# Six tiles held at the head of each stage, the seventh after them: other orders around five norms of a two-block transformer kernel

## The chip, the cores and the metric

The kernel runs on one core of one Trainium2 chip. The metric is the time of one execution on the device in microseconds (us), as the median of several runs. A profile is one further execution, recorded by the hardware profiler. All times below are microseconds.

## The reference

512 tokens of 1024 values, f32, pass through two transformer blocks. What matters here is that each stage begins with an RMS norm, whose result enters one wide matrix product:

```python
def rms_norm(x, g):
    x32 = x.astype(jnp.float32)
    y = x32 * lax.rsqrt(jnp.mean(x32 * x32, axis=-1, keepdims=True) + EPS)
    return (y * g.astype(jnp.float32)).astype(x.dtype)
...
        xn = rms_norm(h, g_mix_pre[i])
        z = xn @ w_in[i]
        conf_ab, q, k, v, f_logit, sc_h, sc_b, sc_c, pool_v = jnp.split(z, SPLIT_IDX, axis=-1)
...
        h = h + rms_norm(mix, g_mix_post[i])
        hn = rms_norm(h, g_mlp_pre[i])
        ff = jnp.square(jax.nn.relu(hn @ w_up[i])) @ w_down[i]
        h = h + rms_norm(ff, g_mlp_post[i])
        gate = jax.nn.sigmoid(rms_norm(h, g_ple_pre[i]) @ w_ple_gate[i])
        e = (p[i] @ w_ple_proj[i]) * gate
        h = h + rms_norm(e, g_ple_post[i])
```

The first mixer holds a forgetting attention, a gated depthwise convolution, a short convolution and a pooling. The second block has a norm, a mixer with sliding-window attention and gated linear attention, another norm, and a gated MLP of width 2816 with a convolution of three taps. So there are five norms in front of products ("1" to "5" below) and three post norms (p1, p2, p3).

## The kernel before

Activations lie transposed: eight groups of 128 channels (index j, or m) by 512 tokens. Every f32 operand of a product is split in a high and a low part that TensorE multiplies as fp32r: x_hi (AH) and x_lo (AL), w_hi (WH) and w_lo (WL). One 128x128 block of weights is three matmuls of 128x512: wh·xh (L1082), wh·xl (L1083), wl·xh (L1084). A tile of the output is 128 channels by 512 tokens in one PSUM bank and needs eight blocks (j = 0 to 7).

**Weights.** They lie in memory in the order of use (NBLK = 1864 blocks) and come in chunks of eight. SyncE loads a chunk (WR, three buffers), ACT rounds it to WH (L1421), DVE subtracts (L1741), or POOL does while the first mixer runs (L2343). Four converted chunks are held (NW). The conversion of chunk c + 3 is told when the first block of chunk c is told (`ahead`), and it waits until chunk c − 1 has been used. It stands in ACT's and DVE's queues behind whatever was told before it.

**The order.** Python code "says" steps (`say`); each engine runs its share of the steps strictly in the order in which they were said, and semaphores join the engines. There is no scheduler: the order of the calls sets everything. Rings of banks (0 to 3) and the single banks 4 to 7 are given out in that order as well.

**Heads.** `head(s, ...)` makes the norm in front of stage s while its products already run. The product is linear, so the factor 1/rms of each token is put on afterwards, when a tile is evicted. x_hi, x_lo and the squares of the eight groups are made one after another; tiles are multiplied j by j with them, several tiles at once ("held"). Before, that is five tiles (three ring banks, P6, P7) with all three matmuls a block, or four tiles in stage 3; ahead of the last j the sums of squares are taken (`sums`), behind it 1/rms is spread over the partitions by a matmul (`spread`), and one more tile follows. DVE computes 1/rms from the sums (`rsqrt_norm`: an estimate by an integer shift and a constant, and Newton steps, twelve small instructions) and copies the spread to RBC (`rbc`, L1784). Then the held tiles are evicted, each with RBC as a factor: in stage 1 q and k (`qk1`, L1813), the forget gate (`forget_in`, L1820, up to `mask1`), glu gates and depthwise convolution (L1895); in stage 2 by `up1` (ACT L1538, POOL L2442, ACT L1543, DVE L1753); in stage 3 by the gates of the ple part; in stage 5 by `ffn_a` (DVE L2268, ACT L1706, DVE L2271 and L2274, ACT L1709) and `ffn_u` (DVE L2283, ACT L1715, DVE L1753).

**Post norms.** `post(n, ...)` sums the squares of the stage's output (ACT L1443 squares, POOL L2353 adds, TensorE L1178 sums over partitions) and adds the normed output to the residual H (`residual`). `warm` is a few matmuls without use on TensorE.

## Time and profile before

| | |
|---|---|
| median of 3 runs | 1488.74 us (1488.62 to 1489.58) |
| the profiled execution | 1483.36 us |
| its span, first to last instruction | 1481.6 us |
| TensorE (PE) busy | 1454.1 us, 98% |
| VectorE (DVE) busy | 798.1 us, 54% |
| ScalarE (ACT) busy | 560.2 us, 38% |
| GpSimd (POOL) busy | 267.8 us, 18% |
| mean granted clock | 0.993 |
| transfers | 129.18 MB, 87 GB/s |

Shares are of the span. SP is SyncE, which issues the transfers. Matmuls overlap in the pipeline of TensorE, so the distance between two starts tells the rate, and not the duration of one.

### The profile page before, as it was taken

How to read it: one execution, taken by the hardware profiler on the slowest of the kernel's cores; microseconds unless marked ns; L12 is line 12 of the kernel's file. 1: busy time of each engine (PE TensorE's matmuls, PEld its weight loads, DVE VectorE, ACT ScalarE, POOL GpSimd, SP SyncE). 2: the span in 40 equal slices, each digit the busy share in tenths (PEclk: the TensorE clock that was granted, in tenths of full speed). 3: DMA queues.
4: the chain of work that ended last, by engine and by line, in shares of the span. 5: the costliest groups of instructions: out<-in, count | busy, mean ns of one | idle time of the engine just before them, and what ended most of it. 6: DMA issues, size and time to landing. Idle time of an engine off the chain costs nothing.

```text
span 1481.6 us, 17750 instructions
## 1 busy us (share of the span) xinstructions
PE 1454.1 (98%) x6978; PEld 1187.9 (80%) x6978; DVE 798.1 (54%) x1155; ACT 560.2 (38%) x829; POOL 267.8 (18%) x180
## 2 busy tenths in 40 slices
PE   9999999999999999999999999999999999999998
PEld 7876768888888887767888888888887888888887
DVE  5687365433333346675767734634435665534554
ACT  5354434522324224443455546322224443323310
POOL 4255344300101012441033201300003000000000
PEclk9999999999999999999999999999999999999999
DMA  6221222332333332221211211323332233332331
GB/s 229 86 71 58 59 70 86 114 100 87 105 94 100 100 91 81 71 71 58 86 43 44 65 50 57 100 85 100 100 100 85 72 114 100 99 100 86 103 100 69
DMA packets 36131, 129.18 MB, mean 87 GB/s; under 512 B 4024, under 2 KB 4280, under 8 KB 36048
## 3 DMA queue, kind: packets, MB, share of 16 engines
q1 hardware_dynamic: 35760, 127.78, 27.8%
q8 instruction: 56, 0.92, 0.3%
q10 hardware_dynamic: 288, 0.26, 0.1%
q14 instruction: 27, 0.22, 0.0%
HBM read 125.91 MB, written 2.10 MB: 86 GB/s over the span
## 4 chain that ended last, share of the span: by engine, by line
PE 88%; DVE 5%; ACT 3%; issue 2%; POOL 2%; DMA 0%; ACTq 0%; DVEq 0%; POOLq 0%
PE P L1082 26%; PE P L1084 26%; PE P L1083 26%; PE P L1341 1%; POOL AC L2353 1%; PE P L1227 1%; DVE P L1895 1%; POOL H L2362 1%; DVE WST L2108 1%; PE P L1123 1%; PE P L1207 1%; PE P L1178 1%; PE P L1303 1%; POOL DD L2353 1%; PE P L1189 0%
## 5 line engine op out<-in xcount | busy, mean ns | idle before, releaser
L1082 PE MATMUL P<-AH,WH 128*128 128x512 f32 x1104 | 443.1, 401 | 10.0 <-issue 4.4
L1084 PE MATMUL P<-AH,WL 128*128 128x512 f32 x1104 | 432.2, 391 | 0.0
L1083 PE MATMUL P<-AL,WH 128*128 128x512 f32 x1104 | 431.9, 391 | 0.0
L1421 ACT ACTIVATE WH<-WR 128x1024 fp32r<-128x1024 f32 x232 | 243.9, 1051 | 339.3 <-PE P L1084 319.4
L1741 DVE TENSOR_TENSOR WL<-WR,WH 128x1024 fp32r<-128x1024 f32 x215 | 278.2, 1295 | 149.5 <-ACT WH L1421 148.9
L1082 PEld LDWEIGHTS P<-AH,WH 128*128 128x128 f32 x1104 | 208.6, 189 | 61.7 <-issue 13.1
L1084 PEld LDWEIGHTS P<-AH,WL 128*128 128x128 f32 x1104 | 208.3, 189 | 44.2
L1083 PEld LDWEIGHTS P<-AL,WH 128*128 128x128 f32 x1104 | 208.6, 189 | 41.9 <-issue 0.7
L1082 PE MATMUL P<-FH,WH 128*128 128x512 f32 x432 | 168.0, 389 | 0.0
L1083 PE MATMUL P<-FL,WH 128*128 128x512 f32 x432 | 168.0, 389 | 0.0
L1084 PE MATMUL P<-FH,WL 128*128 128x512 f32 x432 | 168.0, 389 | 0.0
L1082 PEld LDWEIGHTS P<-FH,WH 128*128 128x128 f32 x432 | 81.1, 188 | 17.0
L1083 PEld LDWEIGHTS P<-FL,WH 128*128 128x128 f32 x432 | 81.1, 188 | 16.8
L1084 PEld LDWEIGHTS P<-FH,WL 128*128 128x128 f32 x432 | 81.1, 188 | 16.7
L2442 POOL TENSOR_TENSOR UB<-TB 128x512 f32<-128x512 f32 x32 | 36.7, 1148 | 193.2 <-ACT TB L1538 193.1
L2353 POOL TENSOR_TENSOR AC<-AC,SQ 128x512 f32<-128x512 f32 x33 | 48.8, 1478 | 126.2 <-ACT SQ L1443 125.1
L1753 DVE TENSOR_TENSOR FL<-UB,FH 128x512 fp32r<-128x512 f32 x32 | 22.1, 692 | 87.3 <-ACT FH L1543 87.3
L2343 POOL TENSOR_TENSOR WL<-WR,WH 128x1024 fp32r<-128x1024 f32 x17 | 41.3, 2432 | 56.1 <-ACT WH L1421 54.8
L1746 DVE SCALAR_TENSOR_TENSOR AL<-H,PM,AH 128x512 fp32r<-128x512 f32 x40 | 43.7, 1105 | 6.9 <-ACT AH L1435 6.3
L1435 ACT ACTIVATE AH<-H,PM 128x512 fp32r<-128x512 f32 x40 | 28.4, 716 | 50.0 <-DVE H L1801 25.0
L1895 DVE SCALAR_TENSOR_TENSOR P<-UP,PM,P 128x512 f32<-128x512 f32 x58 | 43.7, 753 | 1.0
L1706 ACT ACTIVATE SS<-AP,PM 128x512 f32<-128x512 f32 x22 | 18.0, 816 | 59.7 <-DVE AP L2268 59.7
(323 smaller groups left out, 1876.5 us busy)
## 6 DMA issues: line engine op xcount, KB each, us to landing
WR<-in_ws SPq DMA_DIRECT2D x232, 512.0 KB, 3.6
out<-Y SPq DMA_DIRECT2D x8, 256.0 KB, 2.0
H<-in_xT SPq DMA_DIRECT2D x3, 512.0 KB, 8.6
C<-in_const SPq DMA_DIRECT2D x1, 946.5 KB, 11.5
H<-in_xT SPq DMA_DIRECT2D x2, 256.0 KB, 4.2
PR<-in_pT SPq DMA_DIRECT2D x1, 512.0 KB, 4.8
WR<-in_ws SPq DMA_DIRECT2D x1, 384.0 KB, 4.7
WR<-in_ws ACTq DMA_DIRECT2D x1, 128.0 KB, 3.7
```

The lines of the kernel that those rows point to most:

```text
L1082: e.matmul(P, wh, xh, start=start, stop=False)
L1083: e.matmul(P, wh, xl, start=False, stop=False)
L1084: ins = e.matmul(P, wl, xh, start=False, stop=stop)
L1421: e.activation(m.WH[:, c % NW, :], m.WR[:, c % NRAW, :], ACT.Copy).then_inc(*at.up("w_hi", "w_hi", c))
L1435: e.activation(m.AH[:, i, :], m.H[:, i, :], ACT.Copy, scale=m.p(GAIN[s], i)).then_inc(*at.up("x_hi", "x_hi", "A" + s, i))
L1741: e.tensor_tensor(m.WL[:, c % NW, :], m.WR[:, c % NRAW, :], m.WH[:, c % NW, :].bitcast(F32), ALU.subtract).then_inc(*at.up("w_lo", "w_lo", c))
L1746: e.scalar_tensor_tensor(m.AL[:, i, :], m.H[:, i, :], m.p(GAIN[s], i), m.AH[:, i, :].bitcast(F32), ALU.mult, ALU.subtract).then_inc(*at.up ...
L1753: e.tensor_tensor(l, source, h.bitcast(F32), ALU.subtract).then_inc(*at.up("x_lo", "x_lo", kind, j))
L1895: e.scalar_tensor_tensor(P if tap < 30 else m.ACC[:, j, :], u, k, P, ALU.mult, ALU.add).then_inc(*at.up("conv1", "conv1", j, tap))
L2343: e.tensor_tensor(m.WL[:, c % NW, :], m.WR[:, c % NRAW, :], m.WH[:, c % NW, :].bitcast(F32), ALU.subtract).then_inc(*at.up("w_lo_pool", "w ...
L2353: e.tensor_tensor(AC, AC, SQ[:, i % 2, :], ALU.add).then_inc(*at.up("summed", "summed", n, i))
L2442: e.tensor_tensor(m.UB[:, s, :], m.TB[:, s, :], m.TB[:, s, :], ALU.mult).then_inc(*at.up("up1", "up1", f))
```

## The change

The diff has six parts.

- `head` holds six tiles in every stage (four ring banks, P6, P7). Each block is split in two steps: `mm_hi` (wh·xh and wl·xh) needs only x_hi, and `mm_lo` (wh·xl) runs one j behind. Weight conversions are asked for when `mm_lo` comes to a chunk.
- A seventh tile (bank 5) follows by itself. The sums stand behind its second block, the spread behind its sixth, and `rbc` behind its last. The seventh is glu 0's tile in stage 1, a seventh tile of the same product in stages 2, 3 and 5, and the narrow tile of the gk gate in stage 4. All seven are evicted behind it.
- For stage 5, x_hi, x_lo and squares of groups 0 to 5 are said inside the loop over the previous product.
- p1's squares 5 and 6 go to buffers of their own, 7 to the second one of SQ; the seventh add is DVE's.
- The residual add of group 1 is DVE's in all three post norms; it was POOL's.
- The integer shift of the reciprocal root is folded in the next instruction.

```diff
+SUMS = 2
...
+    def narrow(self, name, c0, n, kind):
+        ids = []
+        def step(t, j):
+            if j == 0:
+                ids.append(self.weight(tuple((0, n * q, name, 128 * q, 128, c0, n) for q in range(8))))
+            self.say("mm_narrow", t, ids[0], kind, n, j)
+        return step
+    def wide(self, spec, kind):
+        return lambda t, j: self.block(t, spec[j], (kind, j), j == 0, j == 7)
...
-    def head(self, s, ready, specs):
+    def head(self, s, ready, specs, mid):
...
-        else:
+        elif s != "5":
             make(0)
             make(1)
             rest(0)
-        rest(1)
-        make(2)
-        got = [self.ring() for _ in range(3)] + [self.bank(b) for b in (6, 7)[:len(specs) - 4]]
+        if s != "5":
+            rest(1)
+            make(2)
+        got = [self.ring() for _ in range(4)] + [self.bank(6), self.bank(7)]
+        behind = []
+        def low(j):
+            for t, i in zip(got, behind):
+                if i // CH >= 3:
+                    self.ahead(i)
+                self.say("mm_lo", t, i, (x, j), j == 7)
         for j in range(8):
-            if j == 7:
-                self.sums(s, 0)
-            for m, t in enumerate(got):
-                self.block(t, specs[m][j], (x, j), j == 0, j == 7)
+            ids = []
+            for t, spec in zip(got, specs):
+                i = len(self.plan)
+                if i // CH < 3:
+                    self.ahead(i)
+                self.plan.append(spec[j])
+                ids.append(i)
+                self.say("mm_hi", t, i, (x, j), j == 0)
+            if j:
+                low(j - 1)
+            behind = ids
+            if s == "5":
+                if j < 2:
+                    make(j + 6)
+                    rest(j + 6)
+                continue
             if j < 5:
                 make(j + 3)
             if j < 6:
                 rest(j + 2)
-        b = self.spread(s)
-        out = got + [self.tile(specs[len(got)], [(x, j) for j in range(8)])]
+        low(7)
+        last = self.bank(5)
+        for j in range(8):
+            if j == SUMS:
+                self.sums(s, 0)
+            if j == SUMS + 4:
+                b = self.bank(4)
+                self.say("spread", s, b)
+            mid(last, j)
         self.say("rbc", s, b)
-        return out
+        return got + [last]
...
-        out = self.head("1", ready, [fm(512), fm(640), fm(768), fm(896), fm(256), fm(384)])
+        out = self.head("1", ready, [fm(512), fm(640), fm(768), fm(896), fm(256), fm(384)],
+                        self.wide(fm(0), "A1"))
...
-        spec = tuple((0, 4 * j, "w_in", 128 * j, 128, 1280, 4) for j in range(8))
+        step = self.narrow("w_in", 1280, 4, "A1")
         t = self.ring()
-        self.say("mm_narrow", t, self.weight(spec), "A1", 4)
+        for j in range(8):
+            step(t, j)
         self.say("forget_in", t)
         self.close(t)
         self.beside(self.forget())
         for j in range(2):
-            t = self.tile(fm(128 * j), A)
+            t = self.tile(fm(128 * j), A) if j else out[6]
...
-        out = self.head("2", ready, [fu(f) for f in range(6)])
+        out = self.head("2", ready, [fu(f) for f in range(6)], self.wide(fu(6), "A2"))
         self.say("ple_in")
-        for f in range(6):
+        for f in range(7):
             up(f, out[f])
-        for f in range(6, 8):
-            up(f, self.tile(fu(f), A))
+        up(7, self.tile(fu(7), A))
...
-        out = self.head("3", ready, [fg(m) for m in range(5)])
+        out = self.head("3", ready, [fg(m) for m in range(6)], self.wide(fg(6), "A3"))
         for m in range(8):
-            t = out[m] if m < 5 else self.tile(fg(m), G)
+            t = out[m] if m < 7 else self.tile(fg(m), G)
+            if m == 7:
+                self.say("ple_gated", 6)
+                self.say("square", "p3", 6, 1)
             self.say("ple_gate", m, t)
             self.close(t)
             if 0 < m < 7:
                 self.say("ple_gated", m - 1)
                 self.say("square", "p3", m - 1, 1)
-        for m in (6, 7):
-            self.say("ple_gated", m)
-            self.say("square", "p3", m, 1)
+        self.say("ple_gated", 7)
+        self.say("square", "p3", 7, 1)
...
-        out = self.head("4", ready, [fq(j) for j in range(4)] + [fm(at("ka")), fm(at("va"))])
+        out = self.head("4", ready, [fq(j) for j in range(4)] + [fm(at("ka")), fm(at("va"))],
+                        self.narrow(name, at("gk"), 16, "A4"))
         for j in range(5):
             self.say("qk2", j, out[j])
             self.close(out[j])
-        spec = tuple((0, 16 * j, name, 128 * j, 128, at("gk"), 16) for j in range(8))
-        t = self.ring()
-        self.say("mm_narrow", t, self.weight(spec), "A4", 16)
-        self.say("gk_low", t)
-        self.close(t)
         self.say("va_in", out[5])
         self.close(out[5])
+        self.say("gk_low", out[6])
...
+            if 0 < m < 7:
+                self.say("x_hi", "5", m - 1)
+                self.say("x_lo", "5", m - 1)
+                self.say("square", "5", m - 1, 0)
...
-        out = self.head("5", ready, [fa(0), fa(1), fu(0), fu(1), fa(2), fu(2)])
+        out = self.head("5", ready, [fa(0), fa(1), fu(0), fu(1), fa(2), fu(2)], self.wide(fa(3), "A5"))
...
+        first(3, out[6])
+        second(3, self.tile(fu(3), A))
...
+    def square(self, n, i):
+        SQ, AC = self.sq(n)
+        if n == "p1" and i >= 5:
+            return SQ[:, 1, :] if i == 7 else self.post(n)[1][:, i - 5, :]
+        return AC if i == 0 else SQ[:, i % 2, :]
...
+    def mm_hi(t, i, x, start):
+        c, o = i // CH, (i % CH) * 128
+        P, xh = m.bank[t.bank][:], m.x(*x)[0]
+        part = int(o >= FIRST)
+        w.wait_ge(*(at("w_hi", c) if c else at("w_hi0", part)))
+        w.wait_ge(*at("x_hi", *x))
+        if start:
+            free(t)
+        e.matmul(P, m.WH[:, c % NW, o:o + 128], xh, start=start, stop=False)
+        w.wait_ge(*(at("w_lo", c) if c else at("w_lo0", part)))
+        e.matmul(P, m.WL[:, c % NW, o:o + 128], xh, start=False, stop=False)
+    def mm_lo(t, i, x, stop):
+        c, wh, wl, ends = weights(i)
+        w.wait_ge(*at("x_lo", *x))
+        ins = e.matmul(m.bank[t.bank][:], wh, m.x(*x)[1], start=False, stop=stop)
...
         w.wait_ge(*at("summand", n, i))
-        if i >= 3:
+        if n == "p1" and i >= 5:
+            w.wait_ge(*at("summed", n, 3))
+        elif i >= 3:
             w.wait_ge(*at("summed", n, i - 2))
-        e.activation(AC if i == 0 else SQ[:, i % 2, :], m.summed(n, i), ACT.Square).then_inc(
+        e.activation(m.square(n, i), m.summed(n, i), ACT.Square).then_inc(
...
-        e.tensor_scalar(u.bitcast(I32), v.bitcast(I32), 1, None, ALU.logical_shift_right).then_inc(
-            *at.up("newton", "root1", name))
-        w.wait_ge(*at("root1", name))
-        e.tensor_scalar(y.bitcast(I32), u.bitcast(I32), -1.0, float(0x5F3759DF), ALU.mult, ALU.add).then_inc(
+        e.tensor_scalar(y.bitcast(I32), v.bitcast(I32), -0.5, float(0x5F3759DF), ALU.mult, ALU.add).then_inc(
...
+        if n == "p1" and i == 7:
+            AC = m.sq(n)[1]
+            w.wait_ge(*at("square", n, 6))
+            w.wait_ge(*at("summed", n, 5))
+            e.tensor_tensor(AC, AC, m.square(n, 6), ALU.add).then_inc(*at.up("summed_last", "summed", n, 6))
...
-        if i % 2 == 0:
+        if i % 2 == 0 or i == 1:
             w.wait_ge(*at("normed", n, i))
             e.tensor_tensor(m.H[:, i, :], m.H[:, i, :], u, ALU.add).then_inc(*at.up("h", "h", s, i))
...
-        if i == 0 or i >= 8 - direct:
+        if i == 0 or i >= 8 - direct or (n == "p1" and i == 6):
             return
-        SQ, AC = m.sq(n)
+        AC = m.sq(n)[1]
         w.wait_ge(*at("square", n, i))
         turn()
-        e.tensor_tensor(AC, AC, SQ[:, i % 2, :], ALU.add).then_inc(*at.up("summed", "summed", n, i))
+        e.tensor_tensor(AC, AC, m.square(n, i), ALU.add).then_inc(*at.up("summed", "summed", n, i))
...
-        if i % 2 == 0:
+        if i % 2 == 0 or i == 1:
```

ACT's queue around the second head. TB and FH are the two ACT steps of `up1`, P the bank, WH the conversion of weights. Before, from the fifth held tile on:

```order
L1538 ACTIVATE TB_92<-P7 128x512
L1543 ACTIVATE FH_88<-UB_93 128x512
L1538 ACTIVATE TB_92<-P2 128x512
L1543 ACTIVATE FH_88<-UB_93 128x512
L1421 ACTIVATE WH_53<-WR_52 128x1024
L1538 ACTIVATE TB_92<-P1 128x512
L1543 ACTIVATE FH_88<-UB_93 128x512
```

After, from the sixth on:

```order
L1624 ACTIVATE TB_92<-P7 128x512
L1629 ACTIVATE FH_88<-UB_93 128x512
L1624 ACTIVATE TB_92<-P5 128x512
L1629 ACTIVATE FH_88<-UB_93 128x512
L1506 ACTIVATE WH_53<-WR_52 128x1024
L1624 ACTIVATE TB_92<-P0 128x512
L1629 ACTIVATE FH_88<-UB_93 128x512
```

The first conversion stands behind seven pairs of evictions instead of six.

ACT's queue behind the fifth head. SS4 are the two ACT steps of `ffn_a`, FH2 the one of `ffn_u`. Before:

```order
L1706 ACTIVATE SS4_133<-AP4_132,PM_56 128x512
L1709 ACTIVATE SS4_133<-SS4_133 128x512
L1715 ACTIVATE FH2_129<-GG4_134 128x512
L1421 ACTIVATE WH_53<-WR_52 128x1024
L1706 ACTIVATE SS4_133<-AP4_132,PM_56 128x512
```

After, the same place:

```order
L1792 ACTIVATE SS4_133<-AP4_132,PM_56 128x512
L1795 ACTIVATE SS4_133<-SS4_133 128x512
L1801 ACTIVATE FH2_129<-GG4_134 128x512
L1792 ACTIVATE SS4_133<-AP4_132,PM_56 128x512
L1795 ACTIVATE SS4_133<-SS4_133 128x512
L1506 ACTIVATE WH_53<-WR_52 128x1024
```

The fourth `ffn_a` moved ahead of the first conversion.

DVE's queue in the first mixer, from `forget_in` on. FX is the forget gate, UP<-P a glu, P6<-UP the depthwise convolution. Before:

```order
L1820 TENSOR_TENSOR FX_72<-P2,RBC1_59 4x512
L1827 TENSOR_SCALAR FX_72<-FX_72,PM_56 4x512
L1829 SCALAR_TENSOR_TENSOR FX_72<-FX_72 4x512
L1834 SCALAR_TENSOR_TENSOR FX_72<-FX_72 4x512
L1837 SCALAR_TENSOR_TENSOR FX_72<-FX_72 4x512
L1839 TENSOR_SCALAR FX_72<-FX_72 4x512
L1879 TENSOR_TENSOR UP_62<-P3,SG_65 128x512
L1892 TENSOR_SCALAR P6<-UP_62,PM_56 128x512
L1895 SCALAR_TENSOR_TENSOR P6<-UP_62,PM_56,P6 128x512 x5
```

After:

```order
L1911 TENSOR_TENSOR FX_72<-P2,RBC1_59 4x512
L1970 TENSOR_TENSOR UP_62<-P5,SG_65 128x512
L1918 TENSOR_SCALAR FX_72<-FX_72,PM_56 4x512
L1920 SCALAR_TENSOR_TENSOR FX_72<-FX_72 4x512
L1983 TENSOR_SCALAR P6<-UP_62,PM_56 128x512
L1986 SCALAR_TENSOR_TENSOR P6<-UP_62,PM_56,P6 128x512 x4
L1925 SCALAR_TENSOR_TENSOR FX_72<-FX_72 4x512
L1928 SCALAR_TENSOR_TENSOR FX_72<-FX_72 4x512
L1930 TENSOR_SCALAR FX_72<-FX_72 4x512
L1986 SCALAR_TENSOR_TENSOR P6<-UP_62,PM_56,P6 128x512
```

Glu 0 and five steps of its convolution now stand between the steps of the forget gate.

## Rows read from the trace of the kernel before

**Rows 1.** Timeline of PE in a plain stretch: start, duration, engine, line, operation

```profile
300.10 0.39 PE L1082 MATMUL P<-AH,WH 128*128 128x512 f32 x1
...
317.10 0.39 PE L1082 MATMUL P<-FH,WH 128*128 128x512 f32 x1
```

**Rows 2.** PE's waits (sum, count, longest); one window (busy by engine, PEclk, DMA)

```profile
PE P L1178 <- POOL AC L2353: 5.3, 3, 3.3
PE P L1082 <- DVE AL L1746: 3.4, 2, 1.8
...
604.00:610.00 6.00, 5.03 (x19) 4.25 (x20) 3.19 (x13) 0.00 (x0) 0.92 (x1) 0.72 0.01 3
```

**Rows 3.** Timeline, first head (in brackets: idle before, what ended it)

```profile
6.06 0.72 ACT L1435 ACTIVATE AH<-H,PM 128x512 fp32r<-128x512 f32 x1 [1.16 <-DMA PM<-in_params]
7.71 0.47 PE L1082 MATMUL P<-AH,WH 128*128 128x512 f32 x1 [1.76 <-DVE AL L1746]
11.49 1.23 DVE L1741 TENSOR_TENSOR WL<-WR,WH 128x1024 fp32r<-128x1024 f32 x1 [2.33 <-ACT WH L1421]
39.38 2.85 DVE L1813 SCALAR_TENSOR_TENSOR QAUG<-P,RBC 64x512 f32<-64x512 f32 x4
```

**Rows 4.** Timeline, the forget gate up to the first scores

```profile
59.34 0.68 DVE L1820 TENSOR_TENSOR FX<-P,RBC 4x512 f32<-4x512 f32 x1 [7.81 <-PE P L1144]
60.05 0.47 DVE L1827 TENSOR_SCALAR FX<-FX,PM 4x512 f32<-4x512 f32 x1
63.88 0.68 DVE L1834 SCALAR_TENSOR_TENSOR FX<-FX 4x512 f32<-4x512 f32 x1 [2.64 <-ACT FX L1462]
65.84 2.44 DVE L1839 TENSOR_SCALAR FX<-FX 4x512 f32<-4x512 f32 x1
65.31 2.68 POOL L2343 TENSOR_TENSOR WL<-WR,WH 128x1024 fp32r<-128x1024 f32 x1 [7.25 <-ACT WH L1421]
78.30 0.70 PE L1207 MATMUL P<-KAUG,QAUG 66*128 66x256 f32 x2 [1.07 <-DVE ST L1850]
```

**Rows 5.** Timeline, end of the first post norm and start of the second head

```profile
199.30 5.19 POOL L2353 TENSOR_TENSOR DD<-DD,SQ 128x512 f32<-128x512 f32 x3
206.84 0.17 DVE L1762 TENSOR_SCALAR NR<-NR 128x4 int32<-128x4 int32 x1
212.87 1.76 DVE L1746 SCALAR_TENSOR_TENSOR AL<-H,PM,AH 128x512 fp32r<-128x512 f32 x1
214.73 0.47 PE L1082 MATMUL P<-AH,WH 128*128 128x512 f32 x1 [2.51 <-issue]
```

**Rows 6.** Timeline, evictions behind the second head

```profile
247.50 0.68 DVE L1784 COPY RBC<-P 128x512 f32<-128x512 f32 x1
260.59 0.63 ACT L1543 ACTIVATE FH<-UB 128x512 fp32r<-128x512 f32 x1 [1.18 <-POOL UB L2442]
262.88 0.63 ACT L1543 ACTIVATE FH<-UB 128x512 fp32r<-128x512 f32 x1 [1.17 <-POOL UB L2442]
264.49 1.23 DVE L1741 TENSOR_TENSOR WL<-WR,WH 128x1024 fp32r<-128x1024 f32 x1 [0.26 <-ACT WH L1421]
```

**Rows 7.** Timeline, third head and third post norm

```profile
580.79 0.47 PE L1082 MATMUL P<-AH,WH 128*128 128x512 f32 x1 [2.13 <-ACT AH L1435]
613.96 0.68 DVE L1784 COPY RBC<-P 128x512 f32<-128x512 f32 x1
618.83 4.88 POOL L2353 TENSOR_TENSOR AC<-AC,SQ 128x512 f32<-128x512 f32 x3 [13.91 <-ACT SQ L1443]
636.70 0.27 PE L1178 MATMUL P<-C,AC 128*128 128x1 f32 x1 [1.38 <-POOL AC L2353]
```

**Rows 8.** Timeline, evictions behind the fifth head

```profile
1148.33 0.69 DVE L2268 TENSOR_TENSOR AP<-P,RBC 128x512 f32<-128x512 f32 x1
1164.58 1.23 DVE L1741 TENSOR_TENSOR WL<-WR,WH 128x1024 fp32r<-128x1024 f32 x1 [0.26 <-ACT WH L1421]
1170.48 1.22 DVE L1741 TENSOR_TENSOR WL<-WR,WH 128x1024 fp32r<-128x1024 f32 x1 [1.65 <-ACT WH L1421]
```

More of the change, by code:

```diff
@@ L803, in down @@
                 self.close(t)
-        pairs(range(3, 8))
+        pairs(range(4, 8))
         pairs(range(8, 16))
@@ L1090, in mm @@
             ins.then_inc(*at.up("w_used", "w_used", c))
+    def mm_hi(t, i, x, start):
[13 more added lines that the diff above has]
+        ins = e.matmul(m.bank[t.bank][:], wh, m.x(*x)[1], start=False, stop=stop)
+        if stop:
+            ins.then_inc(*at.up("full", "full", t.id))
+            if ends:
+                at.also(("full", t.id), "w_used", c)
+        elif ends:
+            ins.then_inc(*at.up("w_used", "w_used", c))
     def mm_tokens(got, i, x, kt, nb):
@@ L1131, in mm_values, with mm_narrow @@
             ins.then_inc(*at.up("w_used", "w_used", c))
-    def mm_narrow(t, i, kind, M):
+    def mm_narrow(t, i, kind, M, j):
         c, wh, wl, ends = weights(i)
         P = m.bank[t.bank][0:M, :]
-        free(t)
-        for j in range(8):
-            xh, xl = m.x(kind, j)
-            s = slice(M * j, M * j + M)
-            w.wait_ge(*at("x_hi", kind, j))
-            w.wait_ge(*at("x_lo", kind, j))
-            e.matmul(P, wh[:, s], xh, start=j == 0, stop=False)
-            e.matmul(P, wh[:, s], xl, start=False, stop=False)
-            ins = e.matmul(P, wl[:, s], xh, start=False, stop=j == 7)
-        ins.then_inc(*at.up("full", "full", t.id))
-        if ends:
-            at.also(("full", t.id), "w_used", c)
+        xh, xl = m.x(kind, j)
+        s = slice(M * j, M * j + M)
+        if j == 0:
+            free(t)
+        w.wait_ge(*at("x_hi", kind, j))
+        w.wait_ge(*at("x_lo", kind, j))
+        e.matmul(P, wh[:, s], xh, start=j == 0, stop=False)
+        e.matmul(P, wh[:, s], xl, start=False, stop=False)
+        ins = e.matmul(P, wl[:, s], xh, start=False, stop=j == 7)
+        if j == 7:
+            ins.then_inc(*at.up("full", "full", t.id))
+            if ends:
+                at.also(("full", t.id), "w_used", c)
     def warm_first(t, n):
@@ L1182, in sums @@
             for q in range(4):
-                ins = e.matmul(P[:, q:q + 1], SQ[:, 1, 128 * q:128 * q + 128], one, start=False, stop=True,
+                ins = e.matmul(P[:, q:q + 1], m.square(n, 7)[:, 128 * q:128 * q + 128], one, start=False, stop=True,
                                skip_group_check=True)
@@ L1403, in gn_spread @@
         spread_to(m.bank[t.bank], m.roots("gn", 16)[1][:, 4 * hh:4 * hh + 4]).then_inc(*at.up("full", "full", t.id))
-    run = {"mm": mm, "mm_tokens": mm_tokens, "mm_values": mm_values, "mm_narrow": mm_narrow, "warm_first": warm_first, "warm": warm, "sums": sums, "spread": spread,
+    run = {"mm": mm, "mm_hi": mm_hi, "mm_lo": mm_lo, "mm_tokens": mm_tokens, "mm_values": mm_values, "mm_narrow": mm_narrow, "warm_first": warm_first, "warm": warm, "sums": sums, "spread": spread,
            "scores1": scores1, "turn1": turn1, "values1": values1, "ln_mean": ln_mean, "ln_center": ln_center,
@@ L2308, in down2 @@
             e.tensor_tensor(y, y, o, ALU.add).then_inc(*at.up("y4", "y4", 2, i))
-    run = {"w_lo0": w_lo0, "w_lo": w_lo, "x_lo": x_lo, "rsqrt_norm": rsqrt_norm, "rbc": rbc, "residual": residual, "qk1": qk1,
+    run = {"w_lo0": w_lo0, "w_lo": w_lo, "x_lo": x_lo, "rsqrt_norm": rsqrt_norm, "square": square, "rbc": rbc, "residual": residual, "qk1": qk1,
            "forget_in": forget_in, "forget0": forget0, "forget2": forget2, "mask1": mask1, "scale1": scale1,
```

4 lines of the change are left out of this document (2 added, 2 removed).

## The prediction, made before the changed kernel ran

> **What bounds the kernel now.** I read the engine summary first, then TensorE's timeline, its waits, and the stretches around the five heads. TensorE is busy 98% of the span (the table above). In a plain stretch its matmuls follow each other without a gap: 75 of them start between 300.10 and 317.10, so one takes 0.227, a weight block (three) 0.681, and a tile of eight blocks 5.45 [rows 1]. An edit can therefore gain only where TensorE waits or where its clock is down. The waits, sorted by what ended them, are short: those that touch this change are 3.4 for x_lo at two head starts and 5.3 for POOL's sums of squares at three places [rows 2]. A pause has a second price: in 604 to 610, with a wait of 3.3 in it, the granted clock is 0.72 on average instead of 1.00 [rows 2]: for part of it TensorE runs at the lower of its two levels, 1.2 instead of 2.4 GHz. Such a stretch is 3.4 long in this trace and does half the work, so it costs 1.7. One follows the wait of 2.13 [rows 7] and one that of 3.3, none the one of 1.65 (3.4 less the 1.76 of the first head). I price the waits that I expect, 2.7 and 5, at their length plus 1.7.
>
> The forecast is a sum over places where this order changes. "Ready" is counted on ACT's and DVE's side, "needed" on TensorE's. The base is the profiled execution, 1483.36 (span 1481.6), which is 0.36% under the median of 1488.74; the sum is then added to the median. Every duration below is in microseconds, plus is slower.
>
> **First head and first mixer, +6.0.** The first matmul waits for x_lo 0 (1.76) and starts at 7.71. After, it needs x_hi 0 only (6.06 + 0.72) and starts at about 6.93 [rows 3]. But a round of the six tiles then uses weights with two matmuls a block, so block 8 is wanted after 16 matmuls, near 10.6. Its low half is ready at 11.49 + 1.23 = 12.72 [rows 3]. From 12.87 the other 127 of 144 matmuls end at 41.7. Before, 144 from 7.71 end at 40.4. I take +1.2.
> Then q and k. Before, the sums stand 13 blocks ahead of the end of the six tiles, and the q/k evictions (2.85 for four, 0.71 each) begin at 39.38, under that tile [rows 3]. After, the sums stand after block two of the seventh tile, and RBC is there 4.25 later (eleven small DVE steps of 0.2, a w_lo of 1.2 and the copy of 0.7), just about when the seventh tile ends (six blocks, 4.1). The tokens' tiles, next on TensorE, need the banks that qk1 frees, and nothing has been evicted yet: they wait for two evictions, 1.3, and for one more, 0.7: +2.0.
> Then the forget gate. Its narrow tile follows the values as before, but glu 0's tile (5.45) now stands ahead of it, so its chain starts 5.45 later on TensorE's scale. The chain runs from 59.34 to the mask at 78.2 [rows 4]. In it DVE waits 2.64 for ACT; after, the dwconv steps that the third order excerpt shows there cover this. Scores are thus wanted 3.2 later (1.2 + 2.0) and come 3.2 + 5.45 − 2.64 later: +2.8, beyond the 1.07 that TensorE waits now [rows 4]. In this chain the tensor_scalar of L1839 takes 2.44, that of L1827 on a tile of the same shape 0.47; POOL's w_lo runs 65.31 to 67.99, over nearly all of the first [rows 4]. After, the same w_lo waits for the same ACT step ahead of the chain, so I leave L1839 at 2.44; without the overlap the part is 2.0 less. Bounds for the whole part: +3.5 with that and a little slack, +8.5 if both waits also lower the clock. The Trainium skill, "SBUF — State Buffer", section "Who interferes with whom", states that a tensor_scalar in a two-port mode and a GpSimd instruction exclude each other, and that the later one blocks fully. The slow row fits that; that it is this lock, the trace doesn't show. By the rule, a step told 2.4 later than POOL's conversion would be free of it and this part +4.0.
>
> **First post norm and second head, −3.1.** POOL's last adds take 1.73 each (5.19 for three) up to 204.5 [rows 5]. One moves to DVE, where such a tensor_tensor takes 0.69 [rows 8], and the squares 5 to 7 no longer wait for buffers: the sums start 0.7 earlier. One Newton instruction (0.17) is gone [rows 5], inside the rounding. Head 2 starts without x_lo 0: 214.73 becomes 212.9, −1.8; its wait is the "issue" of 2.51, and the row of x_lo ends just ahead of it [rows 5]. Of the 5.3 for sums of squares, 3.3 are head 3's and 1.38 the third post norm's [rows 2, 7]; the 0.6 left are head 2's, whose sums now lie behind 50 blocks instead of 35: −0.6. The residual add of m = 1 on DVE (0.7) against POOL's shared turn is taken as nothing: it is inside the x_lo that no longer counts; uncovered it is 0.7.
>
> **After the second head, +4.4.** This is the term that I trust most. While ACT and DVE evict the held tiles, no weights are converted: the first order excerpt shows w_hi standing behind all pairs. Before, from RBC (247.50 + 0.68 = 248.18) to the end of the low half (264.49 + 1.23 = 265.72) are 17.54, for six tiles, each 2.29 (260.59 to 262.88) [rows 6]. Seven tiles: 19.83. TensorE holds converted weights for 24 to 25 blocks from the chunk's request, 16.3 to 17.0; its seventh tile ends 0.15 behind RBC, so it runs dry 17.15 after RBC. Before, RBC came with most of the sixth tile still ahead of TensorE, and there was no wait. Wait 2.7, clock 1.7: +4.4. (If that clock stretch stays away, +2.7.)
>
> **Third head to the start of the fourth, −3.5.** The head starts at 580.79 after a wait of 2.13 [rows 7]. I give −0.7 for the low half that the first matmul no longer needs; the 1.4 left are less than the 1.65 that left the clock alone. So its six tiles start near 580.1 and run without the clock stretch; the sums come 50 blocks (34.05) later, near 614.2, with their squares long done: the 3.3 [rows 2] and the stretch behind it go too. But RBC, now at 613.96 + 0.68 = 614.64, comes at 614.2 + 0.9 + 4.25 = 619.35. Behind it stands a chain that does not shrink: gates on DVE and ACT, POOL's adds (three in 4.88, so 1.6 each) [rows 7], w_hi of the next chunk behind square 5, gate 7 and its square; I lay it out to end 16 after RBC, and the sums' result at 17.1, so 636.5. It is 638.7 now (636.70 and two for the sums) [rows 7]. That is −2.2, although TensorE's tiles end some 6.4 earlier than they are needed: most of what the third head wins is waited for again here. Newton −0.2, the warming matmuls at half clock +0.7, head 4's start without x_lo −1.8. Together −3.5. Behind it, the clock stretch at 646.7 may go away: −0.8, half of 1.7. In the fourth head qk2 0 meets RBC 0.4 later.
>
> **Fifth head, +5.4.** The start has no wait any more (six of its eight inputs are made inside the mix2 loop): −1.8, the 1.65 [rows 2, 3] and a little of the first step. RBC against the seventh tile: +0.6. Then the same convoy as after head 2, in longer steps. The first AP starts at 1148.33. Six tiles later w_lo ends at 1165.81, 17.5 on; the next, which stands behind one more AP and its steps, ends at 1171.70 [rows 8]. After, the fourth ffn_a is told ahead of that first conversion (second order excerpt), so the first low half is ready at 1171.70 less the 1.2 of the w_lo that stood between: 22.2 after the first AP. TensorE needs it at 0.8 + 24 blocks (16.35) = 17.1. Wait 4.9 to 5.1, clock 1.7, start and RBC −1.2: +5.4.
>
> **Sum.** 6.0 − 3.1 + 4.4 − 3.5 − 0.8 + 0.4 + 5.4 = +8.8: 1492.2 on the profiled scale, 1497.5 on the median's, 0.6% slower.
>
> **Rivals.** *The convoy never starves TensorE* (the other side). If ACT reaches the first conversion after heads 2 and 5 within 17.1 of RBC, because evictions of seven tiles overlap more closely than the six did, both waits and clock stretches go, 2.7 + 1.7 + 5.0 + 1.7 = 11.0 less: about 1486.5. It decides where the interval RBC to w_lo drops under 17.1. The rows of 2.29 per tile speak against it. Chance 0.10, plus 0.05 for faster in some other way. *The mixer absorbs its slip*: if the scores' tiles leave slack I don't see, +6.0 becomes +1: 1492.5. The 1.07 of wait there now says that there is none. 0.10. *The third post norm's chain grows*: if ACT's squares fall behind POOL's adds in series, that part goes from −3.5 to 0: 1501. 0.10. The forecast has 0.65.
>
> **How the numbers follow.** The three runs lie within 0.07%; 0.2%, 3 us, is about what can be told from no change. The range takes in the mixer's bounds (−2.5, +2.5), the clock stretches (−3.4), and the rivals at 1492.5 and 1501: 1490 to 1503. The rival at 1486.5 is "same" at best or slightly faster. Faster 0.06, same 0.12, slower 0.82.
>
> **What would show it.** Right: TensorE's waits list L1084 or L1082 released by DVE WL or ACT WH for some 2.7 after RBC2 of head 2, and 5 after that of head 5, each with a granted clock near 0.5 behind it; the rows of x_lo at head starts gone; SyncE's transfers early, so that it is conversions and not loads that are late; scores1 of the first mixer waiting for the mask. The third head without a wait before its sums, and one before p3's sums. Wrong: if conversions stay within 17.1 of RBC, or if waits of 2.7 leave the clock at 1.00, the sum loses 4 to 11.

## The result and the profile after

The changed kernel takes 1496.11 us in the median of seven runs (1492.56 to 1500.01), the one before 1488.74 (seven runs, 1488.09 to 1491.35). The ratio is 1.0047, with a 95% interval of 1.0032 to 1.0062: slower by 7.4 us, or 0.5%. The forecast was 1497.5, in 1490 to 1503.

Runs of one kernel differ mainly by the clock that they were granted. The profiled execution of after took 1500.01 at a mean clock of 0.986, the one of before 1483.36 at 0.993. I therefore use a second number beside the ratio, **the span at full clock**: span times mean granted clock, averaged over the runs. It takes half of each stretch at half clock away. Over 29 runs, taken with the first experiments, the kernel before has 1472.5 (single runs scatter by 1.2); over seven the changed one has 1478.6 (0.7). The clock is recorded to 0.001, which is 1.5 of a span, so only averages count here. So the change adds 6.1 at full clock, and the rest is clock: 1.3 by the ratio (7.4 less 6.1), 3.2 by the mean clocks. The measure has a weakness: where TensorE waits inside a stretch at half clock, only half of the wait is counted. In the profile of after, waits of 3.6 lie inside such stretches, in that of before 0.1 (the window view below, length less PE's busy time), so the waits of after are counted too low by up to 1.8.

TensorE's waits after. The columns are sum, count, longest; before they are [rows 2].

```profile
PE P L1263 <- POOL AC L2444: 7.1, 1, 7.1
PE P L1141 <- issue: 4.5, 1, 4.5
PE P L1292 <- DMA KAUG<-FX: 3.6, 1, 3.6
PE P L1160 <- ACT AH L1520: 2.5, 3, 1.3
PE P L1141 <- DVE WL L1827: 2.3, 1, 2.3
...
PE P L1187 <- DVE QAUG L1904: 1.3, 2, 0.9
```

The 3.4 for x_lo and the 3.3 before the third head's sums are gone. In their place stand 7.1 before the third post norm's sums (1.4 before), 4.5 after the fifth head, 3.6 before the first scores (1.1 before) and 2.3 after the second head. Three heads now wait for x_hi, 2.5 in all.

The timeline of after at these places, in order of time. It answers to [rows 3, 4], [rows 6, 7] and [rows 8]:

```profile
12.16 0.50 PE L1162 MATMUL P<-AH,WL 128*128 128x512 f32 x1 [0.56 <-DVE WL L1827]
...
73.26 2.40 POOL L2434 TENSOR_TENSOR WL<-WR,WH 128x1024 fp32r<-128x1024 f32 x1 [7.28 <-ACT WH L1506]
73.37 2.83 DVE L1925 SCALAR_TENSOR_TENSOR FX<-FX 4x512 f32<-4x512 f32 x1
77.48 0.41 DVE L1930 TENSOR_SCALAR FX<-FX 4x512 f32<-4x512 f32 x1
...
258.78 0.69 DVE L1875 COPY RBC<-P 128x512 f32<-128x512 f32 x1
278.07 1.22 DVE L1827 TENSOR_TENSOR WL<-WR,WH 128x1024 fp32r<-128x1024 f32 x1 [0.26 <-ACT WH L1506]
279.44 0.47 PE L1141 MATMUL P<-AH,WH 128*128 128x512 f32 x1 [2.30 <-DVE WL L1827]
...
588.90 0.50 PE L1160 MATMUL P<-AH,WH 128*128 128x512 f32 x1 [1.30 <-ACT AH L1520]
639.51 1.97 DVE L1827 TENSOR_TENSOR WL<-WR,WH 128x1024 fp32r<-128x1024 f32 x1 [1.64 <-ACT WH L1506]
641.40 0.68 DVE L2102 TENSOR_TENSOR Y<-PJ,TB 128x512 f32<-128x512 f32 x1
642.82 1.26 POOL L2444 TENSOR_TENSOR AC<-AC,SQ 128x512 f32<-128x512 f32 x1 [2.42 <-ACT SQ L1529]
644.24 0.98 PE L1263 MATMUL P<-C,AC 128*128 128x1 f32 x4 [7.09 <-POOL AC L2444]
...
1165.83 0.69 DVE L2359 TENSOR_TENSOR AP<-P,RBC 128x512 f32<-128x512 f32 x1
1186.44 1.23 DVE L1827 TENSOR_TENSOR WL<-WR,WH 128x1024 fp32r<-128x1024 f32 x1 [1.64 <-ACT WH L1506]
1187.77 0.47 PE L1141 MATMUL P<-AH,WH 128*128 128x512 f32 x1 [4.49 <-issue]
```

After the second head the low half is ready at 279.29, 19.8 after RBC (259.47), where [rows 6] had 17.5 for six tiles; TensorE had nothing left for 2.30. The weights that it held thus lasted about 17.5 after RBC. After the fifth it is ready 21.8 after the first AP, and the wait is 4.49. The profile puts that wait down to "issue", but the matmul starts 0.1 behind the end of the low half at 1187.67: it is the same wait. Both conversions began on ACT right behind the eviction ahead of them (276.99 and 1185.37, no wait in their rows), so their place in the queue was late, and not a transfer.

Five of the seven stretches at half clock of after, in the window view (length, busy time by engine, granted clock, share of the DMA queues, GB/s):

```profile
78.90:85.70 6.80, 5.32 (x14) 4.29 (x15) 6.05 (x11) 2.84 (x4) 1.10 (x2) 0.50 0.29 80
...
280.30:283.70 3.40, 3.40 (x10) 2.63 (x9) 1.92 (x2) 1.99 (x3) 1.34 (x1) 0.50 0.53 154
642.10:652.30 10.20, 8.06 (x25) 5.92 (x26) 3.63 (x13) 1.86 (x3) 1.26 (x1) 0.50 0.15 51
706.90:713.70 6.80, 6.80 (x22) 5.64 (x21) 3.67 (x3) 3.40 (x3) 0.00 (x0) 0.50 0.26 77
...
1188.20:1191.60 3.40, 3.40 (x10) 2.66 (x9) 2.44 (x4) 1.58 (x2) 0.00 (x0) 0.50 0.50 154
```

With those from 164.2 to 171.0 and from 928.8 to 932.2 the seven are 40.8 long, against six of 3.4 before: at most 20.4 lost instead of 10.2. In this profile every new wait of 2.3 or more has one at its side. But those at 164.2, 706.9 and 928.8 follow no new wait, and the run with the profile had more of them than most: its clock of 0.986 stands against a mean of 0.989 over the seven runs.

### The profile page after: what moved, and what is told of

Its sections match the earlier page's. It is cut to its first block, busy times and chain, and to the rows that moved or that the text cites. A ratio compares the mean times of both kernels' runs of the same rounds, so it can differ in the third digit from the quotient of the medians.

```text
span 1498.2 us, 17669 instructions
## 1 busy us (share of the span) xinstructions
PE 1464.6 (98%) x6978; PEld 1194.8 (80%) x6978; DVE 798.0 (53%) x1149; ACT 560.7 (37%) x829; POOL 259.5 (17%) x175
## 4 chain that ended last, share of the span: by engine, by line
PE 88%; DVE 6%; ACT 3%; issue 2%; POOL 1%; DMA 0%; ACTq 0%; SPq 0%; DVEq 0%; POOLq 0%
PE P L1141 23%; PE P L1142 22%; PE P L1143 22%; PE P L1168 4%; PE P L1160 4%; PE P L1162 4%; PE P L1426 1%; PE P L1312 1%; DVE WL L1827 1%; DVE WST L2199 1%; PE P L1292 1%; PE P L1207 1%; PE P L1263 1%; PE P L1388 1%; POOL UB L2533 0%
## 5 line engine op out<-in xcount | busy, mean ns | idle before, releaser
L1142 PE MATMUL P<-AL,WH 128*128 128x512 f32 x864 | 340.5, 394 | 0.0
L1142 PEld LDWEIGHTS P<-AL,WH 128*128 128x128 f32 x864 | 164.8, 191 | 32.8 <-issue 0.7
L1839 DVE TENSOR_TENSOR FL<-UB,FH 128x512 fp32r<-128x512 f32 x32 | 22.2, 693 | 86.7 <-ACT FH L1629 86.7
L1168 PE MATMUL P<-AL,WH 128*128 128x512 f32 x240 | 60.1, 389 | 0.0
```

Source lines behind the costliest of these rows:

```text
L1142: e.matmul(P, wh, xl, start=False, stop=False)
L1168: ins = e.matmul(m.bank[t.bank][:], wh, m.x(*x)[1], start=False, stop=stop)
L1839: e.tensor_tensor(l, source, h.bitcast(F32), ALU.subtract).then_inc(*at.up("x_lo", "x_lo", kind, j))
```

## The experiments

The theory after the result: the loss has three sources, each a place where work for which TensorE waits is told behind work that has grown. (a) Weights are converted behind seven evictions. (b) The forget gate's narrow tile stands behind glu 0's tile. (c) The third post norm's squares follow an RBC that comes later. The rival: the waits only mark where the clock falls, and moving one makes another. All experiments ran against the kernel before in the same chip time, in three groups (e1 to e4, e5 to e8, e9 to e12). At full clock the kernel before had 1472.5, 1472.3 and 1472.2 in them. The changed kernel itself was measured only at first, seven times, against seven runs of before; an experiment's distance to its 1478.6 goes across chip times. The table has the ratio with its interval and the span at full clock.

| kernel | ratio to before | span at full clock |
|---|---|---|
| before | 1 | 1472.5 |
| after | 1.0047 (1.0032 to 1.0062) | 1478.6 |
| e1_conv | 1.0012 (0.9994 to 1.0029) | 1473.5 |
| e2_head3_old | 1.0064 (1.0045 to 1.0084) | 1477.7 |
| e3_small | 0.9988 (0.9971 to 1.0006) | 1472.1 |
| e4_early_sums | 1.0077 (1.0052 to 1.0101) | 1475.2 |
| e5_inside | 1.0061 (1.0040 to 1.0082) | 1474.8 |
| e6_head1_old | 1.0015 (1.0001 to 1.0029) | 1473.6 |
| e7_conv_h1 | 0.9972 (0.9956 to 0.9987) | 1469.0 |
| e8_best3 | 1.0017 (1.0002 to 1.0033) | 1472.6 |
| e9_two_conv | 0.9979 (0.9963 to 0.9996) | 1469.1 |
| e10_late3 | 0.9943 (0.9923 to 0.9964) | 1467.9 |
| e11_both | 0.9934 (0.9909 to 0.9959) | 1467.9 |
| e12_pool_later | 1.0048 (1.0025 to 1.0070) | 1479.0 |

**e1_conv.** Edits against the changed kernel:

```diff
+    def early(self):
+        self.convert(self.converted + 1)
+        self.rest()
...
         for f in range(7):
             up(f, out[f])
+            if f == 2:
+                self.early()
...
         second(1, out[3])
+        self.early()
```

> The changed kernel with one edit: behind the third held eviction of the second head, and behind the second ffn_u of the fifth, the next chunk of weights is told to be converted, instead of behind all seven. Theory (TensorE runs dry since conversions stand behind the evictions): the waits of 2.3 at 279.4 and of 4.5 at 1187.8 are gone, with the clock stretch of 1.7 behind each, so TensorE's records are 6.8 shorter in waits and up to 3.4 in clock: a ratio to the kernel before of 0.998 to 1.001 where the changed kernel has 1.005. Rival (the evictions are the bound, in whatever order): the ring banks come free 2.3 later, TensorE waits for a bank instead, and the ratio stays at 1.004 to 1.006.

The span at full clock fell by 5.1. TensorE's waits:

```profile
PE P L1270 <- POOL AC L2451: 7.1, 1, 7.1
PE P L1299 <- DMA KAUG<-FX: 3.6, 1, 3.6
...
PE P L1148 <- issue: 2.2, 2, 2.0
```

The 2.3 became 0.63 and the 4.5 became 2.0, and these now belong to the next chunk, whose conversion stands behind the remaining evictions. No wait for a bank came up. So (a) holds: of the 6.8 of wait, 4.0 went (0.2 came up one chunk further on), and the span at full clock lost 5.1. The theory had all 6.8 going; the ratio of 1.0012 lies just above its 0.998 to 1.001, with an interval that reaches into it.

**e2_head3_old.** The third head with the call and the gate loop of before, in a copy of the old `head`:

```diff
-        out = self.head("3", ready, [fg(m) for m in range(6)], self.wide(fg(6), "A3"))
+        out = self.head_old("3", ready, [fg(m) for m in range(5)])
```

> The changed kernel with the third head as before: four tiles with all three matmuls a block, sums ahead of their last group, one tile after, then the gates in the order of before. Theory (the third post norm's chain hangs on the third head's RBC, which comes 5 later with seven tiles): the wait before the post norm's sums falls from 7.1 to about 1.4, the wait of 3.3 before the third head's own sums comes back, the start is 0.8 later; in sum 1 to 2 less waiting, and the total within 2 of the changed kernel. Rival (the p3 wait is a cost that the third head's six tiles add and nothing is given for it): the total is 5 or more under the changed kernel.

```profile
PE P L1303 <- POOL AC L2484: 4.6, 2, 3.3
```

The 4.6 are the 3.3 and 1.4 of before, in place of 7.1. The total at full clock stayed within 1 of the changed kernel: what the new third head saves at its own sums, it gives back at the post norm's, but for the 1 to 2 of waits that the theory named. This is the theory's outcome, and it shows (c): the wait of 7.1 comes with the third head's new order.

**e3_small.** The kernel before with the `square`, `residual` and `rsqrt` parts of the diff alone.

> The kernel before with the small edits alone: buffers for the first post norm's squares 5 to 7 and the seventh add on VectorE, the residual add of group 1 on VectorE, the shift of the reciprocal root folded. Theory: the sums of the first post norm start 0.7 earlier, each root is 0.2 shorter, 1 to 2 less in all, a ratio of 0.9987 to 0.9995. Rival (the moved adds lengthen VectorE's queue where x_lo is awaited): 1.000 to 1.001.

It has 1472.1 at full clock, 0.4 under before, and the ratio's interval holds 1. The direction fits the theory, but no difference is resolved.

**e4_early_sums.** In `head`, the sums and the spread go into the loop over the held tiles:

```diff
-SUMS = 2
+SUMS = {"1": 6, "2": 7, "3": 6, "4": 7, "5": 6}
...
         for j in range(8):
+            if j == SUMS[s]:
+                self.sums(s, 0)
+            if j == SUMS[s] + 1:
+                b = self.bank(4)
+                self.say("spread", s, b)
+                self.say("rbc", s, b)
             ids = []
...
-            if j == SUMS:
-                self.sums(s, 0)
-            if j == SUMS + 4:
-                b = self.bank(4)
-                self.say("spread", s, b)
             mid(last, j)
-        self.say("rbc", s, b)
```

(Where SUMS is 7, spread and RBC are told right behind the held tiles.)

> The changed kernel with the sums of the norms inside the six held tiles (ahead of group 6 in stages 1, 3 and 5, of group 7 in stages 2 and 4), spread and RBC one group of six blocks later, so that RBC comes while the held or the seventh tile is still computed and is earlier by 8 to 14 blocks, 5 to 9. Theory: waits of conversions after heads 2 and 5 shrink by as much as RBC comes earlier, both go to nothing; the wait before the third post norm's sums falls from 7.1 to under 2; the q/k banks are free in time (1.3 gone); a new wait for squares of up to 2 ahead of the early sums. Total 8 to 15 under the changed kernel: a ratio to before of 0.995 to 1.000. Rival (the seventh tile's own length, not RBC, sets the evictions, since the ring is free only behind it): nothing moves after heads 2 and 5, and the ratio is 1.002 to 1.005.

At full clock it gained 3.4, not 8 to 15, and by the ratio, 1.0077 at a mean clock of 0.985, it was no faster than the changed kernel and outside both ranges. After the second head the wait for converted weights is gone, and so are the waits for QAUG; after the fifth 4.5 became 2.5, and before p3's sums 7.1 became 5.9. Its timeline in the third head:

```profile
619.39 0.69 DVE L1879 COPY RBC<-P 128x512 f32<-128x512 f32 x1 [5.07 <-PE P L1278]
...
623.26 1.06 ACT L1510 ACTIVATE WH<-WR 128x1024 fp32r<-128x1024 f32 x1 [3.95 <-PE P L1172]
624.35 1.23 DVE L1831 TENSOR_TENSOR WL<-WR,WH 128x1024 fp32r<-128x1024 f32 x1 [3.14 <-ACT WH L1510]
...
625.53 1.06 ACT L1510 ACTIVATE WH<-WR 128x1024 fp32r<-128x1024 f32 x1 [1.21 <-PE P L1147]
626.62 1.23 DVE L1831 TENSOR_TENSOR WL<-WR,WH 128x1024 fp32r<-128x1024 f32 x1 [1.04 <-ACT WH L1510]
```

RBC is there at 620.1, and then ACT and DVE stand idle behind two conversions that wait for TensorE to use up a chunk; the first gate starts at 627.8. The sums, told after 36 blocks, also met squares that were not ready (4.1 of wait). Both my theory and the rival missed this: an RBC that is there 7.7 ahead of the first gate is of little use while the evictions stand behind conversions that wait.

**e5_inside.** e4 with a callback in the seventh tile's loop that tells one eviction behind each of its first six blocks, in stages 2, 3 and 5:

```diff
             mid(last, j)
+            if evict:
+                evict(j, got)
```

> Early sums as in e4_early_sums, and in stages 2, 3 and 5 the evictions of the six held tiles are told between the blocks of the seventh tile, one behind each of its first six blocks, instead of behind its last. TensorE's order is that of e4. In e4 RBC was there at 620.1 in the third head, and the first gate only at 627.8, behind the conversions that the seventh tile asks for and that wait for TensorE. Theory (what the convoy and the third post norm wait for is the place at which the evictions are told, not RBC): the wait of 2.5 after the fifth head goes, the 5.9 before p3's sums fall to 0 to 1.5. Span less clock loss 6 to 9 under e4's: 1466 to 1469 where before has 1472.5. Rival (RBC and POOL's chain set it): p3's wait stays above 4 and the span less clock loss at 1473 to 1475.

It gained 0.4 only, and p3's wait is 5.6: these are the rival's numbers. ACT in the third head shows why:

```profile
614.67 1.06 ACT L1520 ACTIVATE WH<-WR 128x1024 fp32r<-128x1024 f32 x1 [8.43 <-PE P L1182]
619.72 1.06 ACT L1520 ACTIVATE WH<-WR 128x1024 fp32r<-128x1024 f32 x1 [3.98 <-PE P L1182]
620.79 1.28 ACT L1653 ACT_TABLE_LOAD   x1
```

The first evictions still stand behind a conversion that waits till 619.7, and later ones are strung out between others. In the fifth head 1.8 of wait is left.

**e6_head1_old.** The first head and the place of glu 0 as before:

```diff
-        out = self.head("1", ready, [fm(512), fm(640), fm(768), fm(896), fm(256), fm(384)],
-                        self.wide(fm(0), "A1"))
+        out = self.head_old("1", ready, [fm(512), fm(640), fm(768), fm(896), fm(256), fm(384)])
...
-            t = self.tile(fm(128 * j), A) if j else out[6]
+            t = self.tile(fm(128 * j), A)
```

> The changed kernel with the first head alone as before: five tiles with all three matmuls a block, sums ahead of the last group, the sixth tile after, glu 0's tile behind the narrow one. Theory (glu 0 ahead of the narrow tile delays the mask, seven held tiles delay the q/k banks): the wait of 3.6 for the copied gate rows becomes the 1.1 of before, the waits of 0.9 and 0.4 on QAUG go, and so does the clock stretch of 6.8 at 78.9: 4 to 6 less in waits, ratio to before near 1.001 to 1.002. Rival (the scores' place on TensorE sets it, not the gate chain): no change beyond 1.

```profile
78.38 0.70 PE L1333 MATMUL P<-KAUG,QAUG 66*128 66x256 f32 x2 [1.07 <-DVE ST L1982]
```

It is 5.0 less at full clock; the waits for the gate rows and for QAUG are gone, and 1.07 stands before the first scores as in [rows 4]. The 5.0 is the price of the whole new first head, not of (b) alone: the edit also brings back the old order of the sums and of q and k. By the waits, 2.6 of it are the gate rows (3.63 to 1.07), 1.3 are QAUG and 0.6 the first low half. No run moves glu 0's tile by itself.

**e7_conv_h1.** e1 and e6 together.

> The changed kernel with the first head as before and the conversion told behind the third eviction in the second and fifth. If the terms add, the span less clock loss is 1478.6 less 5.1 (conversion) less 4 to 6 (first head): 1468 to 1470, 3 to 4 under the kernel before, ratio 0.997 to 0.999. Rival (the terms overlap, a wait removed comes back at the third post norm): 1472 or more.

It has 1469.0: the two terms add (5.1 + 5.0 expected, 9.6 measured), and this version beats both kernels, by 0.28% (0.13 to 0.44) the one before. So what is left of the change gains 3.3 at full clock (1472.3 less 1469.0). Of that the small edits are 0.4 by e3, which is not resolved. No run takes the rest apart (heads that start without x_lo, the fifth head's early inputs).

**e8_best3.** e5 and e6 together.

> e5_inside with the first head as before. If the terms add, 4 to 6 under e5: a span less clock loss of 1461 to 1465, a ratio to before of 0.992 to 0.996, with fewer clock stretches as no wait over 2.2 is left but the squares' one in the third head (4.1 in e4).

It has 1472.6, 2.2 under e5, and is no faster than before. The forecast of 1461 to 1465 rested on e5's own, which had failed: its early sums wait for squares (4.1) and p3 still waits 5.6. The first head's half came to 2.2 instead of 4 to 6 as well: with the early sums e5 no longer has the waits for QAUG, so that only the 2.6 for the gate rows were left to gain.

**e9_two_conv.** Against e7, two conversions among the held evictions:

```diff
-            if f == 2:
+            if f in (1, 4):
                 self.early()
...
         second(0, out[2])
+        self.early()
         second(1, out[3])
-        self.early()
         first(2, out[4])
+        self.early()
```

> e7_conv_h1 with two conversions told among the held evictions instead of one: in the second head behind the second and the fifth eviction, in the fifth behind ffn_u 0 and behind the third ffn_a. In e7 the wait had only moved one chunk on: 0.6 at 274.3 and 2.0 at 1176.2, for the chunk behind. Theory: both go, span less clock loss 1466 to 1467 where e7 has 1469.0. Rival (a further chunk is late in its turn, or a bank): 1468 to 1470.

The wait after the second head went, but after the fifth 2.0 became 1.2 and, seven later, 1.5: nothing gained (1469.1), the rival's outcome. The 1.2 is a wait for ffn_u's product GG: a conversion put ahead of an eviction makes that eviction late.

**e10_late3.** Against e7, the conversions asked for in the eighth tile of the third stage are told behind p3's last square:

```diff
     def ahead(self, i):
+        if self.held:
+            return
...
         for m in range(8):
+            if m == 7:
+                self.held = True
...
         self.say("square", "p3", 7, 1)
+        self.held = False
+        self.ahead(len(self.plan) // CH * CH)
+        self.rest()
         return self.post("p3", 1)
```

> e7_conv_h1 with the conversion that stands among the last gates of the third head told behind the last square of p3. In the changed kernel its low half runs 639.5 to 641.5 on VectorE, ahead of the seventh gated product. Theory: the wait before p3's sums, 7.1, falls by 2.0 to 2.5. Rival (POOL's chain of adds sets the sums): under 1 less.

```profile
617.82 0.68 DVE L2159 TENSOR_TENSOR Y<-PJ,TB 128x512 f32<-128x512 f32 x1
...
617.92 1.74 POOL L2501 TENSOR_TENSOR AC<-AC,SQ 128x512 f32<-128x512 f32 x1 [15.77 <-ACT SQ L1586]
...
617.92 9.85 POOL L2501 TENSOR_TENSOR AC<-AC,SQ 128x512 f32<-128x512 f32 x6 [15.77 <-ACT SQ L1586]
622.60 2.64 DVE L2159 TENSOR_TENSOR Y<-PJ,TB 128x512 f32<-128x512 f32 x2
626.51 1.26 POOL L2501 TENSOR_TENSOR AC<-AC,SQ 128x512 f32<-128x512 f32 x1
626.54 1.78 DVE L2159 TENSOR_TENSOR Y<-PJ,TB 128x512 f32<-128x512 f32 x1 [0.70 <-ACT TB L1696]
...
627.92 1.41 PE L1320 MATMUL P<-C,AC 128*128 128x1 f32 x6 [5.08 <-POOL AC L2501]
```

The wait fell from 7.1 to 5.1, as expected. GpSimd's six adds (9.85; the first of them is also shown by itself) now start 1.7 apart, each as soon as the last one is done, where a single one takes 1.26. What is left looks like that chain; no run shortens it. At full clock the total gained 1.1, which is too little: of e7's wait 3.7 lie inside a stretch at half clock and count half, of e10's 0.6. The ratio improved by more, to 0.9943: the stretch at half clock there is 6.8 long instead of the 10.2 of e7.

**e11_both.** e9 and e10.

> e9_two_conv and e10_late3 together. If the terms add: span less clock loss 1464 to 1465, a ratio to before of 0.993 to 0.996.

It has 1467.9, the same as e10 and not 1464 to 1465: e9's conversions give nothing here either. The ratio of 0.9934 (0.9909 to 0.9959) is the lowest of all, but its margin over e10 is not resolved. The profiled run has a clock of 0.996.

**e12_pool_later.** `self.onpool = True` is set behind `forget2` instead of ahead of the narrow tile.

> The changed kernel with GpSimd's share of the weight conversions beginning behind the last step of the forget gate, so that VectorE makes the one that ran on GpSimd from 73.3 to 75.7. Theory (VectorE's step of 2.83 at 73.37 is held up by GpSimd, whose instruction had begun 0.1 earlier): the step takes 0.7, VectorE's conversion 1.2 more, so the copied gate rows and the scores come 0.9 to 1.5 earlier; the wait of 3.6 becomes 2.1 to 2.8. Rival (the step is long by itself there): it stays at 2.8, and the wait grows by 1.2.

This is neither outcome. DVE in e12:

```profile
74.38 1.84 DVE L1925 SCALAR_TENSOR_TENSOR FX<-FX 4x512 f32<-4x512 f32 x1
76.26 1.21 DVE L1928 TENSOR_TENSOR_SCAN FX<-FX 4x512 f32<-4x512 f32 x1
```

GpSimd's conversion still ran from 73.27 to 75.68; I had moved the one ahead of it. DVE's step began 1.0 later than in the changed kernel, and ended at the same time: 76.22 against 76.20. The wait stayed, 3.7 for 3.6. So the step was not tested alone, but it ends 0.54 behind GpSimd's conversion both times.

## Why the prediction was right, point by point

The total, the direction and the order of size held, and so did the waits that it named. By its own steps:

- *First head and mixer, +6.0.* Right in kind, 5.0 by e6. The wait before the scores grew from 1.07 to 3.63 (2.6 for a forecast 2.8), the low half at 12.16 was late as forecast, and q and k cost 1.3 where I had 2.0. The step that I had expected to keep its 2.44 (L1839) took 0.41, but another of the chain took 2.83 in its place. The Trainium skill, "SBUF — State Buffer", section "Who interferes with whom", says that a DVE instruction with two SBUF inputs contends with a GpSimd instruction that reads SBUF. The trace agrees: in two kernels this step, with starts 1.0 apart, ends 0.54 behind GpSimd's conversion. The tensor_scalar, clear of it, took 0.41.
- *First post norm and second head, −3.1.* At full clock the way from p1's sums to the head's start is 1.2 shorter, and the waits of 0.7 before p1's and of 0.6 before the head's sums are gone: −2.5. e3 gives the small edits 0.4, not resolved.
- *After the second head, +4.4.* Right: 19.8 from RBC to the low half for a forecast 19.83, wait 2.30 for 2.7, and a clock stretch of 3.4 behind it in this profile.
- *Third head to fourth, −3.5.* Mis-sized: −0.7. From the third head's start to the fourth's, before took 65.6 (580.79 to 646.43) and after 65.7 (588.90 to 654.65); only the 0.8 less of wait at the third head's start was gained. RBC came 39.1 after the head's start, forecast 39.25, and the wait of 7.1 was foreseen as 6.4. The term that failed is RBC to the sums' result: 17.1 forecast, 19.8 measured (628.03 to 647.82). In it, the last square was ready 17.3 after RBC where I had 16: the low half took 1.97 and a gated product 1.26 beside GpSimd's adds. From there to the result it took 2.5 where I had 1.1, since the sums ran at half clock. The part thus came out near the rival "the third post norm's chain grows" (0 in place of −3.5), but not by that rival's mechanism, ACT's squares falling behind.
- *Clock at 646.7, −0.8.* Wrong in sign: stretches at 706.9 and 928.8 came instead. They are no mark of the six tiles: e3, which has the heads of before, has a stretch of 10.2 at 697.6 and one of 3.4 at 922.9.
- *Fifth head, +5.4.* Right: no wait at the start, 21.8 for 22.2, wait 4.49 for 4.9 to 5.1, clock stretch 3.4.

Cut at the starts of the heads, with half of every stretch at half clock taken away, the two profiles and the forecast compare like this. The forecast's column is its parts without their clock terms; the third head's −3.5 also holds 5.1 of clock that before loses there, against 2.4 that it left after (1.7, and 0.7 for the warming matmuls). What a head's start gains stands in the row that ends with it.

| from the start of | forecast | measured |
|---|---|---|
| the kernel to the second head | +3.5 | +2.1 |
| the second head to the third | +1.4 | +0.8 |
| the third head to the fourth | −0.1 | +0.1 |
| the fourth head to the fifth | −1.4 | −1.7 |
| the fifth head to the end | +5.5 | +5.0 |
| sum | +8.9 | +6.4 (6.1 over all runs) |

So the forecast was 8.9 of waits and −0.1 of clock; measured are about 6 of waits (up to 8 with the waits inside half-clock stretches) and 1 to 3 of clock. That the total came out within 1.4 of the forecast is partly luck: the waits were taken too high, and the clock too low by about as much. The third head shows the clock's part: before's three stretches of 3.4 there came back as one of 10.2, where I had two of the three go.

The rule that I had for the clock, a stretch of 3.4 behind a wait of 2.1 or more, did not hold in the very trace that I read it from. The stretch at 639.8 follows the wait of 1.38 of [rows 7], those at 158.6 and 206.3 follow none above 0.7, and the wait of 2.51 ahead of the second head [rows 5] has none behind it.

What stays open: what decides the clock stretches that follow no wait (164, 700 to 710, 910 to 930). They stand in most of the profiles with other lengths, the mean clock differs from run to run in the same kernel, and no experiment isolated them.

## What to carry to other kernels

With strict queues, count the time between what asks for a weight conversion and the TensorE work that still covers it: a group of evictions longer than that (about 17.5 here) starves the bound engine, and splitting two such groups with one conversion each gave back 5.1. An earlier input is worth little if its consumers are told behind instructions that wait for the bound engine (the third head in e4 and e5). A saved wait ahead of a serial chain on another engine is given back at the chain's end, unless the chain itself gets shorter (e2, e10).
